# An expert's second matrix in one 4 MB transfer, and the downward products by pairs of experts

## The reference, cut to what matters

```python
# h: normed tokens (256, 2048); comb: (256, 32), zero outside each token's two experts
a = einsum('nd,edf->nef', h, w1)          # w1, w3: (32, 2048, 512) float32
b = einsum('nd,edf->nef', h, w3)
y = einsum('nef,efd->nd', silu(a) * b * comb[..., None], w2)   # w2: (32, 512, 2048)
```

## Time and profile before

| | |
|---|---|
| median of three runs | 1342.96 us |
| the profiled execution's own time | 1342.74 us |
| its span | 1341.0 us |
| TensorE matmul busy | 974.8 us, 73% of the span |
| DMA moved | 480.57 MB, mean 358 GB/s |
| chain that ended last | PE 50%, DMA 46%, SyncE's queue 2% |
| mean granted clock of TensorE | 0.872 of 2.4 GHz |

### The profile page before, as it was taken

The page is one execution under the profiler, slowest core; times in us unless marked ns, Lnnn a source line. Parts: engine busy times, 40 slices in busy tenths (PEclk is TensorE's granted clock), DMA queues, the critical chain, the costliest instruction groups (busy, mean ns, idle before and its releaser), DMA issues.

```text
span 1341.0 us, 19016 instructions
## 1 busy us (share of the span) xinstructions
PE 974.8 (73%) x8278; PEld 649.8 (48%) x8278; DVE 329.6 (25%) x505; ACT 306.5 (23%) x553; POOL 71.5 (5%) x48
## 2 busy tenths in 40 slices
PE   8999999999999983656477375536736654674647
PEld 6987888888888651333134133313412421341222
DVE  5557967544753200100010010001001000100101
ACT  6545555545542410001001000100100010010000
POOL 0000242500010020000000000000000000000000
PEclk9999999999999987877788687878868777896888
DMA  8745646544697999999999999999999999999998
GB/s 297 243 133 170 205 157 219 179 160 144 189 421 296 382 430 437 432 426 437 432 433 429 436 432 430 435 433 435 427 435 434 429 435 432 431 431 435 433 428 330
DMA packets 65052, 480.57 MB, mean 358 GB/s; under 512 B 7256, under 2 KB 11760, under 8 KB 47984
## 3 DMA queue, kind: packets, MB, share of 16 engines
q1 hardware_dynamic: 64976, 479.94, 87.2%
q10 hardware_dynamic: 32, 0.01, 0.0%
HBM read 477.84 MB, written 2.10 MB: 358 GB/s over the span
## 4 chain that ended last, share of the span: by engine, by line
PE 50%; DMA 46%; SPq 2%; DVE 1%; issue 1%; ACT 0%; DVEq 0%; ACTq 0%
DMA ring<-w_dram 46%; PE ps L1631 12%; PE ps L1366 9%; PE ps L1368 9%; PE ps L1367 9%; PE ps L1669 5%; SPq L482 1%; PE ps L1384 1%; SPq L398 1%; PE ps L1586 1%; PE ps L1400 0%; PE ps L1478 0%; DMA xs<-x_dram 0%; PE ps L1434 0%; PE ps L1410 0%
## 5 line engine op out<-in xcount | busy, mean ns | idle before, releaser
L1631 PE MATMUL ps<-ring,side_buf 128*32 128x256 f32 x3968 | 264.1, 432 | 247.0 <-DMA ring<-w_dram 247.0
L1631 PEld LDWEIGHTS ps<-ring,side_buf 128*32 128x32 f32 x3968 | 150.7, 124 | 364.9 <-issue 308.1
L1366 PE MATMUL ps<-w_split,zT_half 128*128 128x512 f32 (+2 forms) x572 | 219.9, 384 | 0.1
L1368 PE MATMUL ps<-w_split,zT_half 128*128 128x512 f32 (+2 forms) x572 | 217.0, 379 | 0.0
L1367 PE MATMUL ps<-w_split,zT_half 128*128 128x512 f32 (+2 forms) x572 | 216.9, 379 | 0.0
L888 DVE TENSOR_TENSOR w_split<-raw_buf,w_split 128x1024 fp32r<-128x1024 f32 (+2 forms) x144 | 180.4, 1270 | 138.4 <-ACT w_split L601 137.7
L1669 PE MATMUL ps<-ring,side_buf 128*32 128x512 f32 x960 | 124.3, 676 | 97.4 <-DMA ring<-w_dram 97.4
L601 ACT CAST w_split<-raw_buf 128x1024 fp32r<-128x1024 f32 (+2 forms) x144 | 144.3, 1019 | 109.2 <-PE ps L1368 109.0
L1266 DVE TENSOR_TENSOR xs<-xs,ps 128x512 f32<-128x512 f32 x56 | 38.5, 687 | 489.8 <-PE ps L1598 489.7
L825 ACT ACTIVATE side_buf<-ps,st 128x256 f32<-128x256 f32 x16 | 6.7, 470 | 542.9 <-PE ps L1631 542.9
L1669 PEld LDWEIGHTS ps<-ring,side_buf 128*32 128x32 f32 x960 | 36.8, 123 | 179.6 <-issue 179.6
(11 more groups left out here) (197 smaller groups left out, 500.3 us busy)
## 6 DMA issues: line engine op xcount, KB each, us to landing
ring<-w_dram SPq DMA_DIRECT2D x56, 4096.0 KB, 25.0
ring<-w_dram SPq DMA_DIRECT2D x72, 2048.0 KB, 21.3
raw_buf<-w_in_dram SPq DMA_DIRECT2D x47, 1024.0 KB, 5.0
raw_buf<-w_out_dram SPq DMA_DIRECT2D x16, 1024.0 KB, 5.7
spare<-w_dram SPq DMA_DIRECT2D x2, 2048.0 KB, 8.5
ring<-w_dram SPq DMA_DIRECT2D x4, 1024.0 KB, 15.4
ring<-w_dram SPq DMA_DIRECT2D x8, 512.0 KB, 13.9
raw_buf<-w_in_dram SPq DMA_DIRECT2D x4, 608.0 KB, 5.5
```

The lines of the kernel that those rows point to most:

```text
L1366: mm(b, zhi(c)[:, t], wh, start=(c == 0), stop=False)
L1368: last = mm(b, zlo(c)[:, t], wh, start=False, stop=(c == C - 1))
L1631: last = mm(ps[part, up, pair * WIDE:(pair + 1) * WIDE], h_e[:, c, slots], w[m][:, cc * NB + h * WIDE:cc * NB + (h + 1) * WIDE], start=(c ...
```

## The change

Three parts.

**Loads.** An expert's whole w2 comes in one `load_matrix` of 4 MB, 32 KB per partition, into two neighbouring slots. For that the layout of w2 on the partitions changes from two halves of (p, 2 rows) to (p, 4 rows). This holds for teams 0 to 6. The last team still loads chunks of 2 MB and the twelve pieces, now as halves of the new layout.

**Downward products.** `down` goes over two pairs of experts. For each pair it waits for both matrices and goes over four row chunks j, four column blocks n and the two experts. The last team's first half is done by `down_by_halves` in the old order.

**Upward products.** As w2's rows lie differently, `up` reads its moving operand permuted: instead of 256 contiguous columns a tile takes two neighbouring float32 out of every four.

```diff
-FIRST_FILLS = [1 + sum(k % RING == slot for k in range(RING + EXTRA, TEAM_CHUNKS)) for slot in range(RING)]
+FIRST_FILLS = [1 + sum(k % RING == slot for k in (*range(RING + EXTRA, UP_CHUNKS), *range(UP_CHUNKS, TEAM_CHUNKS, 2)))
+               for slot in range(RING)]
...
-    return 3 if slot % 2 == 0 else 1
+    return 3 if slot % 2 == 0 else 0
...
-        w2_v = w2.rearrange("l e (h p s) n -> (l e) h p (s n)", h=2, s=2)
+        w2_v = w2.rearrange("l e (p s) n -> (l e) p (s n)", s=J)
...
-                    src = w2_v[bass.ds(number * TEAM + m, 1), half]
+                    src = w2_v[bass.ds(number * TEAM + m, 1), :, half * 4096:(half + 1) * 4096]
...
             def load_matrix(k, number):
                 pair, up, m = k // 8, k // 4 % 2, k // 2 % 2
-                src = (w3_v if up else w1_v)[bass.ds(number * TEAM + 2 * pair + m, 1)]
+                if k < UP_CHUNKS:
+                    src = (w3_v if up else w1_v)[bass.ds(number * TEAM + 2 * pair + m, 1)]
+                else:
+                    src = w2_v[bass.ds(number * TEAM + (k - UP_CHUNKS) // 2, 1)]
...
             def team(it, number):
-                matrices(it, number)
-                for k in range(UP_CHUNKS, TEAM_CHUNKS):
-                    sp.wait_ge(ring_used, it * TEAM_CHUNKS + (k - RING + 1))
-                    load(k, number)
+                matrices(it, number, TEAM_CHUNKS)
...
-                        src = w2_v[(TEAMS - 1) * TEAM + m, 1].rearrange("p (s n) -> p s n", s=2)
+                        src = w2_v[(TEAMS - 1) * TEAM + m, :, 4096:8192].rearrange("p (s n) -> p s n", s=2)
...
-            for k in range(RING + EXTRA, TEAM_CHUNKS):
-                sp.wait_ge(ring_used, k - RING + 1 if k >= 2 * RING + EXTRA else k - RING - EXTRA + 1)
+            for k in range(RING + EXTRA, UP_CHUNKS):
+                sp.wait_ge(ring_used, k - RING - EXTRA + 1)
                 load(k, 0)
+            for k in range(UP_CHUNKS, TEAM_CHUNKS, 2):
+                sp.wait_ge(ring_used, (k + 1 - RING if k + 1 >= 2 * RING + EXTRA else k + 1 - RING - EXTRA) + 1)
+                load_matrix(k, 0)
...
-                            last = mm(ps[part, up, pair * WIDE:(pair + 1) * WIDE], h_e[:, c, slots],
-                                      w[m][:, cc * NB + h * WIDE:cc * NB + (h + 1) * WIDE],
+                            last = mm(ps[part, up, pair * WIDE:(pair + 1) * WIDE].rearrange("p (q s) -> p q s", s=2),
+                                      h_e[:, c, slots],
+                                      w[m][:, cc * NB:(cc + 1) * NB].rearrange("p (q h s) -> p h q s", h=2, s=2)[:, h],
                                       start=(c == 0), stop=(c == C - 1))
...
-            def down(it, halves):
-                for half in halves:
-                    ks = [UP_CHUNKS + TEAM * half + m for m in range(TEAM)]
-                    w = [landed_now(it, k) for k in ks]
-                    for j in (2 * half, 2 * half + 1):
+            def down(it):
+                for pair in range(PAIRS):
+                    experts = (2 * pair, 2 * pair + 1)
+                    for m in experts:
+                        landed_now(it, UP_CHUNKS + 2 * m)
+                    for j in range(J):
                         for n in range(4):
-                            for m in range(TEAM):
+                            for m in experts:
                                 part = slice(SLOTS * m, SLOTS * (m + 1))
+                                at = j % 2 * D + n * NB
                                 last = mm(ps[part, 4 + n, :], hm_lhsT(m, j),
-                                          w[m][:, j % 2 * D + n * NB:j % 2 * D + (n + 1) * NB],
+                                          ring[:, chunk_slot(UP_CHUNKS + 2 * m + j // 2), at:at + NB],
                                           start=(j == 0), stop=(j == J - 1))
                     last.then_inc(ring_used, TEAM)
```

More of the change, by code:

```diff
@@ L106, in first_landed @@
     return 16 * ((k - EXTRA) // RING + 1)
-FIRST_FILLS = [1 + sum(k % RING == slot for k in range(RING + EXTRA, TEAM_CHUNKS)) for slot in range(RING)]
+FIRST_FILLS = [1 + sum(k % RING == slot for k in (*range(RING + EXTRA, UP_CHUNKS), *range(UP_CHUNKS, TEAM_CHUNKS, 2)))
+               for slot in range(RING)]
 def fills(slot):
-    return 3 if slot % 2 == 0 else 1
+    return 3 if slot % 2 == 0 else 0
 def chunk_landed(k):
     slot = chunk_slot(k)
-    before = k // RING if slot % 2 == 0 else 0
-    return 16 * (FIRST_FILLS[slot] - fills(slot) + before + 1)
+    return 16 * (FIRST_FILLS[slot] - fills(slot) + (k // RING if slot % 2 == 0 else 0) + 1)
 def build(nc, x, norm1_g, w_in, q_norm_g, k_norm_g, idx_k_ln_w, idx_k_ln_b, ret_norm_g, w_out,
@@ L453, in _, with matrices @@
                     load_first((q - FLAT_FREE - EXTRA) % RING)
-            def matrices(it, number):
-                for k in range(0, UP_CHUNKS, 2):
+            def matrices(it, number, chunks):
+                for k in range(0, chunks, 2):
                     sp.wait_ge(ring_used, it * TEAM_CHUNKS + (k + 1 - RING + 1))
@@ L461, in team @@
             def team(it, number):
-                matrices(it, number)
-                for k in range(UP_CHUNKS, TEAM_CHUNKS):
-                    sp.wait_ge(ring_used, it * TEAM_CHUNKS + (k - RING + 1))
-                    load(k, number)
+                matrices(it, number, TEAM_CHUNKS)
             def last_team(it):
-                matrices(it, TEAMS - 1)
+                matrices(it, TEAMS - 1, UP_CHUNKS)
                 for k in range(UP_CHUNKS, LAST_GROUP):
@@ L1659, in turn_gate, with down_by_halves @@
                 last.then_inc(gate_turned, 1)
-            def down(it, halves):
-                for half in halves:
-                    ks = [UP_CHUNKS + TEAM * half + m for m in range(TEAM)]
-                    w = [landed_now(it, k) for k in ks]
-                    for j in (2 * half, 2 * half + 1):
+            def down(it):
[4 more added lines that the diff above has]
+                    for j in range(J):
                         for n in range(4):
-                            for m in range(TEAM):
+                            for m in experts:
                                 part = slice(SLOTS * m, SLOTS * (m + 1))
+                                at = j % 2 * D + n * NB
                                 last = mm(ps[part, 4 + n, :], hm_lhsT(m, j),
-                                          w[m][:, j % 2 * D + n * NB:j % 2 * D + (n + 1) * NB],
+                                          ring[:, chunk_slot(UP_CHUNKS + 2 * m + j // 2), at:at + NB],
                                           start=(j == 0), stop=(j == J - 1))
                     last.then_inc(ring_used, TEAM)
+            def down_by_halves(it):
+                w = [landed_now(it, UP_CHUNKS + m) for m in range(TEAM)]
+                for j in range(2):
+                    for n in range(4):
+                        for m in range(TEAM):
+                            part = slice(SLOTS * m, SLOTS * (m + 1))
+                            last = mm(ps[part, 4 + n, :], hm_lhsT(m, j),
+                                      w[m][:, j * D + n * NB:j * D + (n + 1) * NB], start=(j == 0), stop=False)
+                last.then_inc(ring_used, TEAM)
             def first_team():
@@ L1704, in between @@
                 pe.wait_ge(hm_T_ready, it + 1)
-                down(it, range(2))
+                down(it)
             def last_down(it):
@@ L1710, in last_down @@
                 pe.wait_ge(hm_T_ready, it + 1)
-                down(it, (0,))
+                down_by_halves(it)
                 pe.wait_ge(gate_T_ready, it + 2)
```

## The result

The changed kernel takes 1348.36 us, the median of six runs (1346.63 to 1349.69); the kernel before took 1342.68 in the same rounds. The ratio is 1.0040, 95% interval 1.0030 to 1.0049: slower by 5.7 us, clear of the 0.2%. Forecast were 1341.8 and "within 0.2%"; the time lies in the stated range of 1339 to 1352, near what the rival of the short cover gave (1349).

A forecast was written before the change was run, and what follows sets the result against it. The prediction took DMA transfers in the experts' stage as the bound: 1342.74 us, loads -1.1, downward products 0, upward products 0, gave 1341.6; with the median 0.2 above the profiled run, 1341.8 us, range 1339 to 1352.

The forecast's parts named there:

- the rival of the short cover: Slot refill in each team: transfers start after 2.9 us, or a longer slow stretch; about 1 us a team, 1349; chance 0.11.
- Loads: w2 loads of seven teams: 4 MB instead of 2 MB transfers save 0.17 us per 16 MB, taken as -1.1 us.
- Downward products: TensorE's products with w2: a pair takes 14.1 us at full clock instead of 7.07 a half; second pairs 15.6 to 17.0.
- 17.9 to 19.3 us after the landing, against 19.5 us: Second pair: freed slots are in transfer again 17.9 to 19.3 us after its landing, before the next group lands at 19.5.
- downward products 0: Term of the sum: doubled TensorE time for products with w2 adds 0 us, as the DMA engines just stay busy.
- the cover: Time freed slots have to be under transfer again before the other group has landed; groups land every 19.5 us at most.
- warm from the gather: First pair of downward products: starts at full clock after the gather, ends 859.9, leaving 5.2 us before the 865.1 landing.
- the start-up bounds: Restart of idle DMA engines after an issue: 0.9 to 2.9 us until the full rate; 1.9 taken.
- Half an array: Rival at the second pair: two tiles do not wake the clock, 27.3 us a pair; 1412 up to 1480 us; chance 0.13.
- The strided read: Upward products' permuted operand: forecast cost 0; as rival 1.5 times the burst, 12 us in all, 1353; chance 0.05.

The follow-up runs named there:

- the loads alone: Changed kernel with its 4 MB loads and strided read, but downward products over halves on four tiles again (numbers wrong, same work): 1341.53 us, ratio 0.9991.
- second half padded: Kernel before with eleven unread matmuls behind the second half of the downward products, ahead of its slots' release: 1353.50 us, ratio 1.0088.
- clock kept up: Changed kernel with five unread matmuls behind the release of the first pair, filling idle time ahead of the second: 1346.71 us, ratio 1.0028.
- padded less: Kernel before with six unread matmuls behind the second half of the downward products, ahead of its slots' release: 1342.62 us, ratio 1.0003.
- the run with 2 MB chunks: Changed kernel with w2 loaded in 2 MB chunks again, products still by pairs of experts: 1349.12 us, ratio 1.0051.
- the rolling order: Changed kernel with downward products reordered so experts overlap one after another and each expert's slots are released when it is done: 1341.83 us, ratio 0.9991.

## Why the prediction was wrong

**Loads: right.** -1.1 us forecast; -0.9 us between the medians for the loads alone, and 38.77 us for the window with w2's groups in the changed kernel.

**Downward products: right in their length.** Two tiles take as long as four. The weight loads of the second pair, two a step now, answer to the earlier trace rows:

```profile
868.34 0.22 PEld L1675 LDWEIGHTS ps<-ring,side_buf 128*32 128x32 f32 x2 [0.64 <-issue]
...
873.44 0.13 PEld L1675 LDWEIGHTS ps<-ring,side_buf 128*32 128x32 f32 x2 [0.62 <-issue]
873.87 0.13 PEld L1675 LDWEIGHTS ps<-ring,side_buf 128*32 128x32 f32 x2 [0.30 <-issue]
```

The pairs took 13.93 us at the full clock (14.1 forecast), the second ones 15.3 to 16.8 in six teams and 13.93 in the seventh (15.6 to 17.0 forecast for all). The doubling that the Trainium skill gives ("TensorE: Matmul & The Clock Gate", Part 3) holds.

**The step that failed is the comparison of "17.9 to 19.3 us after the landing, against 19.5 us".** On it rested the term "downward products 0" of the sum, which came out at some 6.6 us (5.7 us slower in spite of the 0.9 us from the loads). Both sides were mis-sized, and the second one more. I counted the cover to the next *landing*, which is when the last of the group's bytes is there. The DMA engines run out of work earlier. The windows of the changed kernel around the hole, columns as in the earlier trace rows, with the release at 884.35 and the landing at 886.95:

```profile
883.00:884.00 1.00, 1.00 (x8) 0.14 (x3) 0.00 (x0) 0.00 (x0) 0.00 (x0) 1.00 0.99 426
884.00:885.00 1.00, 0.35 (x2) 0.00 (x0) 0.00 (x0) 0.61 (x2) 0.00 (x0) 1.00 0.46 197
885.00:886.00 1.00, 0.00 (x0) 0.00 (x0) 0.00 (x0) 1.00 (x3) 0.00 (x0) 1.00 1.60 459
886.00:887.00 1.00, 0.00 (x0) 0.00 (x0) 0.00 (x0) 0.98 (x2) 0.00 (x0) 1.00 0.28 98
887.00:888.00 1.00, 0.92 (x12) 0.47 (x16) 0.00 (x0) 0.74 (x1) 0.00 (x0) 0.53 1.22 492
```

The rate falls from 426 to 197 GB/s from 884 on, 16.6 us after the landing of 867.38 and 3 us ahead of the next, and is back at 887, 2.65 us after the release. Against 433 GB/s the three microseconds from 884 to 887 lack 1.3 us; the next landing was 2.1 us late. Single windows of 1 us scatter (311 to 492 GB/s in the kernel before from 700 to 712), so each of these edges is good to about 1 us.

The first side came out at 16.84 + 2.65 = 19.5 us, not above the 19.5 us that it was held against. What made the loss is the second side: the queued work ended at 16.6 us and not at 19.5. In other bursts the rate left its level at 16.2 us (second half padded, fifth team, 66 GB/s from 1003), 15.2 us (clock kept up, third team, 66 GB/s from 748) and even 14.4 us (second half padded, second team, 164 GB/s from 649, where no landing was late); it was back 2.4 to 2.9 us after the release. So the cover is not one figure. Worked out from the hole above, an estimate, bursts are too long from 16.6 - 2.65 = 14 us on, and not from 17.2. The runs agree: bursts up to 14.0 us (padded less) and the second pairs of 13.93 us (clock kept up) cost nothing, though two first pairs of that length lost 0.6 and 0.4 us; bursts of 15.3 to 17.2 us cost between nothing and 2.5 us each.

**A second omission: the first pair.** I let it start "warm from the gather" in all teams. In the first team it starts after 4.31 us of idle time and took 16.49 us; its release too was late, by 1.9 us at the landing behind the next. The trace of the kernel before has the like: the first half of that team took 9.02 us instead of 7.07, behind 4.79 us of idle time. In the seventh team the first pair took 15.62 us.

**The forecast went to the wrong side of its own rival.** The short cover was priced at 1 us a team, 7 us in all, 1349; the traces give 7 us in all, unevenly spread, and 1348.4. That the price met the time is partly luck. The rival named a start of 2.9 us or a longer slow stretch, and neither came: with the issue the start took 2.65 us where the rival has 3.3, and the slow stretch was about as long as before. What came was a cover shorter than the time between landings, behind some of the pairs, first ones too. The rival's chance was 0.11, with 1.9 us, the middle of the start-up bounds, in the forecast. With 0.2 us between the two numbers compared, and one of them a landing, that was no ground for 0.66.

**The other rivals.** Half an array does wake the clock: the second pair above goes from steps of 0.86 to 0.43 us within the burst, and the rival's 27.3 us never occur. The slow stretch lasted 5.9 us here (867.5 to 873.4), about as long as the longest before, whose loss of 2.9 us is 5.8 us at half the rate. The Trainium skill ("TensorE: Matmul & The Clock Gate", Part 1) lets the clock follow how busy the engine is, and the trace agrees. The strided read cost 7.46 instead of 7.11 us, 5% and not 50%, and nothing of the end: ratio 1.0002 by itself.

**What stays open.** Not each late release makes a late landing. With 2.6 to 2.7 us from the end of the burst to the next landing, the changed kernel lost 2.1 and 1.9 us behind it; with 3.0 us nothing in the sixth team, though its rate fell to 164 GB/s as well (1120 to 1121), and the run with 2 MB chunks once nothing with 2.5 us, though its rate there stayed below 330 GB/s for five microseconds, of which three are shown:

```profile
1001.00:1002.00 1.00, 0.90 (x6) 0.00 (x0) 0.00 (x0) 0.07 (x1) 0.00 (x0) 1.00 0.61 262
1002.00:1003.00 1.00, 0.00 (x0) 0.00 (x0) 0.00 (x0) 1.00 (x3) 0.00 (x0) 1.00 1.16 328
1003.00:1004.00 1.00, 0.00 (x0) 0.00 (x0) 0.00 (x0) 0.99 (x3) 0.00 (x0) 1.00 0.75 229
```

It would fit that the engines that are ahead of the others can wait without delaying the last one, on which a landing depends. That is an argument, and not shown; the views here don't tell the 16 engines apart. The late landing in the second team of the kernel before, which no late release explains, stays open with it.

## What to carry to other kernels

In a kernel bound by transfers, more work on another engine can be free up to a point and cost behind it, here 0 to 2.5 us a time; to find the point, count from the release of a buffer to the point where the transfer engines run out of queued work, and take that some microseconds (here 2.5 to 5) ahead of the landing that the chain of waits shows. When work moves from four tiles to two, ask first what is released at its end. If the work must be long, release its buffers one by one and fill the gap ahead of it: the rolling order did the same products without a loss.

## What the runs showed of the hardware

- The DMA engines together left the full rate some 3 us ahead of the landing of the last queued group (2.5 to 5 us in the bursts read here, in windows of 1 us), and were back at it 2.4 to 2.9 us after the release that refilled the queue.
- 128x512 float32 products took 0.43 us a step at the full clock for two column tiles as for four, and two tiles at work were enough to bring the clock back from 1.2 to 2.4 GHz, 5.9 us into the burst at 867.51.
- Reading float32 in pairs at a step of four cost 5%: 7.46 for 7.11 us. The Trainium skill's rule of two hits in a line of sixteen bytes ("SBUF — State Buffer", Door 1) gives no cost; the measurement decides, and the cost is far under the 1.5 times of the nearest row.
- 16 MB in pieces of 32 KB took 38.73 us, in pieces of 16 KB 38.87 to 38.90, whether in transfers of 2 or 4 MB.
- A loop with 22 more matmuls a team got an idle time of 4.79 to 5.89 us on "issue" in TensorE in each of six teams, and 86 transfers of instructions instead of 31; one with 11 more got neither.
